# Delta mixer's betas by tokens: inputs stationary, eight high and eight low weight columns moving, in a two-block kernel on one core

## What is computed

```python
h = _rmsnorm(x, norm_pre)                       # [256, 1024]
cols = h @ w_in
(dn_qkv, dn_z, dn_b, dn_a, gm_uv, ...) = _split_cols(cols)   # dn_b, dn_a: 4 columns each
qkv = silu(_causal_dwconv(dn_qkv, conv_w))      # 1536 columns, width-4 convolution over tokens
beta = sigmoid(dn_b)                            # one number per token and head
g = -exp(a_log) * softplus(dn_a + dt_bias)      # one number per token and head
o = _gated_delta_chunked(q, k, v, g, beta)
```

## Time and profile before

| | us |
|---|---|
| median of 3 runs (1398.5 to 1398.68) | 1398.57 |
| the profiled execution: its time | 1398.59 |
| its span in the trace | 1396.8 |
| PE busy in the span | 1386.2 (99%) |
| PEld busy | 1231.8 (88%) |
| DVE busy | 907.7 (65%) |
| ACT busy | 735.9 (53%) |

### The profile page before, as it was taken

One profiled execution on the slowest core, in us unless ns is written; L12 is line 12 of the kernel. 1 busy time (PEld: TensorE's weight loads), 2 busy tenths in 40 slices (PEclk: granted clock), 3 DMA queues, 4 the chain that ended last, 5 costly groups with the idle time before them and its releaser, 6 DMA issues.

```text
span 1396.8 us, 21530 instructions
## 1 busy us (share of the span) xinstructions
PE 1386.2 (99%) x8348; PEld 1231.8 (88%) x8348; DVE 907.7 (65%) x1162; ACT 735.9 (53%) x908; POOL 72.8 (5%) x113
## 2 busy tenths in 40 slices
PE   9999999999999999999999999999999999999998
PEld 8999989888888888899888888888889999888886
DVE  5565798575576665766666656656667676666656
ACT  7566664343365444557554445544445468544444
POOL 1000010000020000010210000000000002200000
PEclk9999999999999999999999999999999999999999
DMA  8543431265545555451465554755555400555552
GB/s 327 196 172 121 173 130 61 91 224 183 183 158 204 181 190 201 153 210 61 169 257 196 193 183 178 251 201 180 180 186 199 157 32 1 215 192 186 201 183 90
DMA packets 34862, 239.13 MB, mean 171 GB/s; under 512 B 4010, under 2 KB 4154, under 8 KB 7152
## 3 DMA queue, kind: packets, MB, share of 16 engines
q1 hardware_dynamic: 33072, 231.46, 46.5%
q0 software_dynamic: 1296, 6.15, 1.2%
q10 hardware_dynamic: 432, 0.66, 0.1%
HBM read 236.11 MB, written 1.08 MB: 170 GB/s over the span
## 4 chain that ended last, share of the span: by engine, by line
PE 97%; ACT 1%; DVE 1%; issue 0%; POOL 0%; POOLq 0%; ACTq 0%; DVEq 0%
PE ps L736 22%; PE ps L706 16%; PE ps L708 16%; PE ps L707 16%; PE ps L744 12%; PE ps L1037 3%; PE ps L1011 2%; PE ps L1021 2%; PE ps L1363 1%; PE ps L3009 1%; PE ps L645 1%; PE ps L3017 1%; PE ps L3020 1%; PE ps L3186 1%; PE ps L827 1%; PE ps L1357 0%
## 5 line engine op out<-in xcount | busy, mean ns | idle before, releaser
L412 DVE TENSOR_TENSOR low<-raw,high 128x2048 fp32r<-128x2048 f32 x211 | 479.6, 2274 | 228.2 <-ACT high L406 225.7
L406 ACT ACTIVATE high<-raw 128x2048 fp32r<-128x2048 f32 (+1 forms) x213 | 403.0, 1894 | 80.1 <-PE ps L708 74.2
L736 PE MATMUL ps<-nt,high 128*128 128x512 f32 x1344 | 320.1, 390 | 0.0
L736 PEld LDWEIGHTS ps<-nt,high 128*128 128x128 f32 x1344 | 249.0, 188 | 49.8
L744 PEld LDWEIGHTS ps<-nt,low 128*128 128x128 f32 x1344 | 167.5, 189 | 3.6
L744 PE MATMUL ps<-nt,low 128*128 128x256 f32 x1344 | 168.6, 283 | 0.0
L706 PE MATMUL ps<-high,hth 128*128 128x512 f32 x320 | 124.5, 389 | 0.0
L707 PE MATMUL ps<-low,hth 128*128 128x512 f32 x320 | 124.5, 389 | 0.0
L708 PE MATMUL ps<-high,htl 128*128 128x512 f32 x320 | 124.5, 389 | 0.0
L706 PE MATMUL ps<-nt,high 128*128 128x256 f32 x400 | 114.0, 285 | 0.0
L708 PE MATMUL ps<-nt,low 128*128 128x256 f32 x400 | 113.0, 282 | 0.0
(11 more groups left out here) (436 smaller groups left out, 2048.4 us busy)
## 6 DMA issues: line engine op xcount, KB each, us to landing
raw<-in_stream SPq DMA_DIRECT2D x214, 1024.0 KB, 4.8
late<-in_w POOLq DMA_DIRECT2D x1, 2048.0 KB, 9.4
scr<-bias_by_distance POOLq DMA_DIRECT2D x1, 2048.0 KB, 15.1
scr<-in_mem SPq DMA_DIRECT2D x2, 512.0 KB, 4.5
raw<-in_stream SPq DMA_DIRECT2D x4, 256.0 KB, 6.3
raw<-in_stream SPq DMA_DIRECT2D x2, 512.0 KB, 7.7
x<-in_x SPq DMA_DIRECT2D x1, 1024.0 KB, 8.3
scr<-scr SPq DMA_DIRECT2D x8, 128.0 KB, 2.3
```

The lines of the kernel that those rows point to most:

```text
L406: nc.scalar.activation(high_of(t, slice(0, n)), raw[t % SLOTS][:, 0:n], ACT.Copy).then_inc(w_high, 1)
L412: nc.vector.tensor_tensor(low_of(t, slice(0, n)), raw[t % SLOTS][:, 0:n], high_of(t, slice(0, n)).bitcast(F32), ALU.subtract).then_inc(w_l ...
L736: last = nc.tensor.matmul(r3(bank, 2), w[:, k, P * j:P * j + P], nt[:, :, k, :], start=first and k == 0, stop=not first and k == KC - 1, s ...
```

## The change

The product for `dn_b` and `dn_a` is turned round: the tokens' inputs are stationary (128 tokens of one chunk of features), and weight columns move. ACT rounds only the 8 real columns of each chunk ([128, 8, 8]); DVE writes what is left of them into the 8 columns behind them of the same `high` tile, where zeros were before. PE then takes, for 2 halves of the tokens and 8 chunks, one product of `nth` with 16 columns (8 high, 8 low) and one of `ntl` with the 8 high columns: 32 matmuls. The result has tokens on partitions already; DVE copies the first 8 columns per half out of the bank and adds the other 8. The two transposes, their semaphore and the copy on line 2404 are gone. The DMA of the tile is as before.

```diff
@@ split_high, split_low @@
+        def decay_columns(tile):
+
+            chunks = tile[:, 0:KC * P].rearrange("p (k w) -> p k w", k=KC)
+            return chunks[:, :, 0:2 * DN_H], chunks[:, :, 2 * DN_H:4 * DN_H]
...
+            if i is None and PLAN[t] == "ba":
+                nc.scalar.activation(decay_columns(high_of(t))[0], decay_columns(raw[t % SLOTS])[0], ACT.Copy)\
+                    .then_inc(w_high, 1)
+                return
...
+            if i is None and PLAN[t] == "ba":
+                rounded, rest = decay_columns(high_of(t))
+                nc.vector.tensor_tensor(rest, decay_columns(raw[t % SLOTS])[0], rounded.bitcast(F32),
+                                        ALU.subtract).then_inc(w_low, 1)
+                return
@@ pe_plain @@
+            elif kind == "D":
+                w = slot(t, KC, P)[0]
+                for j in range(TT):
+                    at = 4 * DN_H * j
+                    for k in range(KC):
+                        nc.tensor.matmul(out_[:, at:at + 4 * DN_H], nth[:, k, P * j:P * j + P], w[:, k, 0:4 * DN_H],
+                                         start=k == 0, stop=False, skip_group_check=True)
+                        last = nc.tensor.matmul(out_[:, at:at + 2 * DN_H], ntl[:, k, P * j:P * j + P], w[:, k, 0:2 * DN_H],
+                                                start=False, stop=k == KC - 1, skip_group_check=True)
@@ DVE @@
             dve_step(dve, "ba")
-            bank_read("ba", nc.vector.tensor_copy(d_bat, read_bank(dve, "ba")[0:2 * DN_H, 0:S]))
+            parts = r3(read_bank(dve, "ba")[:, 0:4 * DN_H * TT], TT)
+            ch.link(nc.vector.tensor_copy(r3(d_ba, TT), parts[:, :, 0:2 * DN_H]))
+            bank_read("ba", nc.vector.tensor_tensor(r3(d_ba, TT), r3(d_ba, TT), parts[:, :, 2 * DN_H:4 * DN_H], ALU.add))
...
                 if j == 1:
-                    dve.wait_ge(dn_bas, 1)
-                    ch.link(nc.vector.tensor_copy(d_ba, ps[3][:, 0:16]))
@@ PE @@
-            pe_plain(pe, "ba", "N")
+            pe_plain(pe, "ba", "D")
             for j in range(6):
                 pe_plain(pe, f"dn{j}", "F")
-                if j == 0:
-
-                    wait_bank(pe, "ba")
-                    for t in range(TT):
-                        last = nc.tensor.transpose(ps[3][:, 8 * t:8 * t + 8], d_bat[:, P * t:P * t + P],
-                                                   ident[0:2 * DN_H, 0:2 * DN_H])
-                    last.then_inc(dn_bas, 1)
```

More of the change, by code:

```diff
@@ L84 @@
 GATE_AND_UP = {f"f{f}{part}{i}" for f in range(4) for part in "gu" for i in range(FT)}
-USED = {"ba": KC * P, "ng": KC * P, "uq0": 1536, "uq1": 1536, "uq2": 1536}
+USED = {"ng": KC * P, "uq0": 1536, "uq1": 1536, "uq2": 1536}
 TILE = {n: i for i, n in enumerate(PLAN)}
@@ L1228, in build @@
         d_os, d_om, d_or = tiny(PAIRS), tiny(PAIRS), tiny(PAIRS)
-        d_bat = dn["kb"][0:2 * DN_H, 0:S]
         n_gt = ns["gt"][0:3 * NSA_H]
@@ L1250, in build @@
          dn_t, dn_u, dn_uc, dn_wc, dn_o0, dn_sc, dn_vnd, dn_osum, dn_out,
-         dn_level, dn_tap0, dn_bas) = (
+         dn_level, dn_tap0) = (
             s_("dn_" + n) for n in ("conv", "act", "turn", "tok", "sum", "ready", "fm", "fa", "fd",
@@ L1254, in build @@
                                     "lm", "p", "pc", "y", "t", "u", "uc", "wc", "o0", "sc", "vnd",
-                                    "osum", "out", "level", "tap0", "bas"))
+                                    "osum", "out", "level", "tap0"))
         KEPT, FREE = bank_of("dn4"), bank_of("dn5")
```

## The result

The changed kernel takes 1401.38 us (median of 17 executions, 1397.93 to 1403.22), the kernel before 1398.23 (17 executions, 1397.46 to 1398.68): ratio 1.0018, interval 1.0012 to 1.0025. Measured again it was 1400.56 us (11 executions, 1398.16 to 1402.61) against 1398.00 (21 executions, 1397.31 to 1399.81): 1.0015, interval 1.0006 to 1.0024. By the medians the change costs 3.15 and 2.56 us, by the ratios some 2.5 and 2 us, and what it does to the spread is as large: the first 17 executions of before lie within 1.2 us, those of the changed kernel over 5.3 us. The forecast was 1398.9, with 1398.0 to 1400.6.

A forecast was written before the change was run, and what follows sets the result against it. PE was taken to bound the kernel: 3.58 us of new products less 2.88 us of old and 0.41 us of transposes gives +0.29, so 1398.57 + 0.29 = 1398.86, say 1398.9 us; range 1398.0 to 1400.6 us.

The forecast's parts named there:

- PE bounds the kernel, and the account is PE's: Whole kernel: PE busy 1386.2 of 1396.8 us, so the edit is worth what it changes in PE's queue.
- 24 products taken out at 0.120 us, the transposes at 0.41, 32 put in at 0.112: PE from ba to the start of dn1: 3.58 - 2.88 - 0.41 = +0.29 us at an even clock.
- ACT, DVE and DMA give and take nothing: Around ba: smaller splits, earlier DMA, DVE's bank read and the removed copy were claimed to be worth nothing.
- the detour: Behind dn2, 164.59 to 188.93 us: chain leaves PE through ACT and DVE, claimed to shift as PE does.
- the old fall: Behind the 20 one-column products, 612.26 to 615.68 us: PE's clock drops from 2.4 to 1.2 GHz, costing 1.50 us.
- The clock falls behind the new `ba`, 2 in 3: At dn0: 32 thin products in a row make the granted clock fall there too, chance 2/3, costing 1.50 us.
- So the fall costs 3.42 - 16 x 0.120 = 1.50 us: Behind the one-column products: 16 products pass in 3.42 us at the lower clock; 1.50 us taken as a fall's price.
- rival (5): Clock fall in dn0 lasting two spells, the existing one staying: 0.29 + 2 x 1.50 = +3.29 us, 1401.9 us, chance 0.03.
- It comes in each execution, at the same place: Fall behind the one-column products claimed to repeat every execution, since four times before agree within 0.18 us.
- the new fall paid for by the loss of the old one: Clock falls in dn0, no longer behind the one-column products: +1.50 - 1.50, total staying +0.29 us, chance 0.42.
- Rival (3): Thin loads pass at 0.060 us, then dn1 waits for DVE's bank read: -0.35 us, 1398.2 us, chance 0.08.
- the same: Whole kernel: change within 0.2% or 2.8 us, 1395.8 to 1401.4 us, not told from no change; chance 0.96.

The follow-up runs named there:

- wide: Changed kernel with all 32 thin products of the tile ba moving 128 columns instead of 16 and 8, extra results unread: 1398.93 us, ratio 1.0006.
- before_wide: Kernel before plus 32 products of 128 moving columns behind the 24 of ba, results unread: 1401.56 us, ratio 1.0023.
- stack_order: Changed kernel with ba redone as 16 products of 256 tokens, high and low columns stationary, and ACT and DVE work reordered: 1397.80 us, ratio 0.9996.
- half: Changed kernel with 16 thin products instead of 32, leaving out those of the inputs' low part: 1398.03 us, ratio 0.9997.
- mixed: Changed kernel with the 32 thin products spread among those of dn0, three behind each group of three: 1398.80 us, ratio 1.0002.
- before_thin: Kernel before plus 32 products of 16 moving columns behind the 24 of ba, results unread: 1403.15 us, ratio 1.0036.
- after_2: Changed kernel, unaltered, measured again with a second profile: 1400.56 us (11 executions), ratio 1.0015.
- after: Changed kernel itself, first measurement and profile: median 1401.38 us (17 executions), ratio 1.0018; profiled execution 1402.63 us.
- after_3: Changed kernel, unaltered, run once more for a third profile: 1402.75 us (1 execution).
- filled: Kernel before with the 20 one-column products that sum squares moving 128 columns of ones instead: 1397.85 us, ratio 0.9998.

## Why the prediction was wrong

- *PE bounds the kernel, and the account is PE's.* Right.
- *24 products taken out at 0.120 us, the transposes at 0.41, 32 put in at 0.112.* Right: +0.29 forecast, +0.29 measured in `wide`, where the clock stays.
- *ACT, DVE and DMA give and take nothing.* Right at `ba`: the detour shifted by 4.10 us, as PE did. It doesn't hold at the other place, where DVE takes back part of what PE saves when the old fall is gone.
- *The clock falls behind the new `ba`, 2 in 3.* Right in kind, and as a chance not contradicted: it did in all three profiles, but five of the first 17 executions are too fast for it.
- *"So the fall costs 3.42 - 16 x 0.120 = 1.50 us".* This is the step that failed, as the term of the sum that was mis-sized. The price was taken from the only fall in the trace, behind a stretch of 2.3 us. Behind 3.58 us the lower level lasted 6.8 us and cost 2.99 us. I had written that case down as rival (5), two such spells with the old one staying, and gave it 0.03 with no better reason than that one spell had been seen. The profiled execution is that rival, at 1402.63 us where it said 1401.9, since it also has the 0.8 us of the first microseconds.
- *"It comes in each execution, at the same place".* Wrong. That rested on four times of before within 0.18 us. Over more executions they lie 1.2 us apart or more, and falls behind the one-column products come in some profiles (the kernel before, `before_wide`, `stack_order`, two of three of the changed kernel) and not in others (`wide`, `half`, `mixed`, `before_thin`, `after_2`), whose one-column products are the same. The case that carried most of the forecast, the new fall paid for by the loss of the old one (0.42), came in the profiles of `after_2` and `before_thin`, and not in those of `after` and `after_3`. The shift alone doesn't decide it: in `before_wide` the one-column products come 3.8 us later than in before and the old fall is there, in `half` 0.1 us later and it is not. No profile has a fall at a third place while PE still has work. And where the old fall was gone it didn't pay: in `after_2` 3.03 us of lower clock at `ba` stand against 1.1 us regained.
- *Rival (3), DVE's read holds `dn1` back.* Not met in the changed kernel; met in `half`, with 1.04 us of waiting. Its price of 0.35 us was too high, since the second product of `dn1` needs 0.34 us behind the read, not 0.17.
- *What "the same" meant.* All cases but one were put inside 0.2% because each was priced by single spells. The median of +3.15 us, 0.22%, lies just beyond that bound, with its interval from 0.12 to 0.25% on both sides of it.

What decides in one execution whether and when the clock falls, and for how long, stays open: no run here sets it. The median cost of thinness is 1.5 us in `before_thin` and some 2 to 3 us in the changed kernel, with 32 products in both. The profiles agree on 3 us at `ba` and differ in the old fall; how the executions without a profile divide isn't known.

## What to carry to other kernels

Before turning a product round so that few columns move, count the loads: here each product of a long run of them costs 0.11 us whether it moves 8 or 128 columns, so the edit must lower the number of products, and 24 to 32 could not. Keep thin products apart from one another by wide ones, or let them move columns that nobody reads, where they would run for microseconds in a row; in the profiles here both kept the clock, and neither cost anything that could be told from no change. When the trace shows a costly event once, price a stronger cause by more than one such event, and don't take it for fixed in time from a handful of equal times. Follow what its loss would save to the next wait: of 1.50 us saved on PE only 1.1 us reached the end.

## What the hardware showed unexpectedly

- The granted clock falls to its lower level, 1.2 GHz, with PE busy for every microsecond: behind 32 products of 16 and 8 columns for 6.8 us, and behind 20 of one column for about 3.4 us in five of the ten profiles that have them. The Trainium skill, page "TensorE: Matmul & The Clock Gate", section "Why this matters for your kernels", names idle gaps of PE between bursts of matmuls as what lowers throughput within a kernel; the same page's section "HAM oscillation — how this bites in real kernels" puts the cost on waits for DMA between bursts. The runs here show the fall without any gap.
- In the changed kernel it falls while the thin products still run, and they slow down too, from 0.112 to 0.213 us from start to start. A page of 40 slices doesn't show it; a stretch of 6 us does.
- The kernel's first microseconds differ from execution to execution (the same 16 transposes in 2.03 us in `half` and 3.20 us in the changed kernel), while the stretches' clock column reads 1.00 there. In `filled`, unchanged up to there, `ba` starts 0.83 us later than in before.
